# Masking the diagonal blocks of stick-breaking attention after the arithmetic instead of in the score copy

## The chip, the cores and the metric

The kernel runs on one core of one Trainium2 chip. Each run gives the time of the whole program on the device in microseconds (us). Three runs of the kernel before were timed, and one execution was profiled. TensorE (PE in the profile) multiplies matrices, VectorE (DVE), ScalarE (ACT) and GpSimd (POOL) work on tiles, SyncE (SP) issues most of the DMA transfers. Each engine runs its own list of instructions in order and waits for the others by semaphores. SBUF is the working memory, PSUM the memory that TensorE writes.

## The reference

One layer of an encoder: a layer norm, an input projection, two attention branches merged by gates, an output projection, a mixture of 64 experts and a final norm, for 1024 prompt rows and 64 sample rows with a cache of 128 keys. The change is in one branch, stick-breaking attention, with 8 heads of 128 columns:

```
z = jnp.einsum('bqhd,bkhd->bhqk', q, k).astype(F32) / math.sqrt(SB_HEAD_DIM)
mask = k_pos[None, :] < q_pos[:, None]
log_keep = jnp.where(mask, jax.nn.log_sigmoid(-z), 0.0)
after = lax.cumsum(log_keep, axis=3, reverse=True) - log_keep
log_w = jnp.where(mask, jax.nn.log_sigmoid(z) + after, 0.0)
w = jnp.where(mask, jnp.exp(log_w), 0.0)
return jnp.einsum('bhqk,bkhd->bqhd', w.astype(v.dtype), v)
```

The mask is strict: a query sees only keys before its own position.

## The kernel before

The program has stages with barriers between them: the mixer (input projection, both attention branches and their merge), a bridge (output projection, norm, router, shared expert), the experts, and the last norm. The change is in the mixer, which works head by head: first `attention(h)`, then `hgrn(h)`, the other branch.

**Units.** Scores stand with the keys on the partitions and the queries along the columns. A head has 14 units, one for each tile of 128 keys against a group of queries, listed by `attention_units`. Units 0 to 7 are queries 512 to 1023 against key tiles 7 down to 0, units 8 to 11 are queries 0 to 511 against tiles 3 down to 0, unit 12 is the 64 sample rows against themselves, and unit 13 is the same rows against the cached keys. A unit holds only the columns that can see its keys: units 0 and 8 are 128 columns wide, 1 and 9 256, 2 and 10 384, the rest 512, units 12 and 13 64. Where keys and queries meet (units 0 to 3, 8 to 11 and 12, entry 5 of the unit's tuple), the first `kr` columns are a diagonal block that needs the mask. That is 9 units of 14 in a head and 72 in all; in units 0, 8 and 12 the whole width is the diagonal block.

**One unit, step by step.** TensorE computes the scores into PSUM (`scores`, L580). VectorE brings them to SBUF as `z` (`front`, L986 and L988). In a diagonal unit this is a copy of the columns behind the block and, on the block, an addition of `cap`, a constant tile of 0 where the key is visible and -1e30 where it isn't. ScalarE takes abs, exp and ln of it (L779, L781, L783). VectorE adds max(z, 0), which gives minus log_keep, in `l` (`middle`, L997). GpSimd splits it in a high part (a cast, L1253) and a low part (a subtraction, L119 on `spl_m`). TensorE sums over the keys with a triangular matrix into PSUM (`sums`, L597 and L598) and later adds the rest of the tile for the next units (`carry`, L608 and L609). VectorE subtracts the sums from z (`back`, L1005), ScalarE takes the exponential (L789), and TensorE multiplies by the values (`values`, L625). VectorE copies finished outputs away (L1015).

**Order.** The order is written by hand. TensorE runs in step n `scores(n + 3)`, then a piece of the projections of this or the next head (`fill`, L125 to L127, of some 4 us each, absent in some steps), then `carry(n - 1)`, `sums(n)` and `values(n - 1)`. `carry` and the next `sums` wait for `arg_done`, which `back` signals. VectorE runs in step n `front(n + 3)`, `middle(n + 2)`, its part of copies of projections from PSUM (L937), `back(n)`, `outputs(n - 1)`, and in some steps whole-width work of the other branch (L1037 to L1051: its decays, and scans of them). GpSimd splits units, splits weights for the projections (L119 on `w_mix_low`), and from the second head on merges the head before (`merge`, L1230 and L1232 behind unit 3, L1236 behind unit 10, L1239 behind unit 11). In the last head there is no next head to project for, so several of TensorE's steps have no projection between their waits.

Two constant tiles matter: `before`, 1 where the key is visible and 0 elsewhere, and `cap`, made from it.

Of the kernel before, what the change touches and what calls it, by code (L numbers as in the profile page):

```python
# [17 lines left out]
ALU = mybir.AluOpType  # L18
# [307 lines left out]
def mixer(nc, a, o, xn_d, st, xT, woh, wol, ps, ident, ones, before, trir, cap, masks, lbc, small, mT_d):  # L326
    S = MixerSteps()
    UN = attention_units()
# [4 lines left out]
    Z, C, PB, OH, KE, SU = (0, 1), 2, (0, 1), 2, 3, 4  # L333
    XD = np.cumsum([0] + DIFFS).tolist()
    XE = np.cumsum([0] + EXPS).tolist()

    with ExitStack() as c:
        def sb(name, shape, dt=F32):
# [11 lines left out]
        with ExitStack() as attention_only:  # L350
            z, l = (attention_only.enter_context(nc.sbuf_tensor(n + "_m", [P, b, 512], F32)) for n, b in (("z", 5), ("l", 3)))
# [8 lines left out]
        epsc, hn = small[:, 0:1], small[:, 1:2]  # L360

        with Phase(nc, "arrived0 arrived1 rounded split mm_done act_read dve_read hn_in ck_in cv_in s_in v_out k_out s_out m_out "
                       "z_done abs_done e_done l_done z_copied sp_done hi_done lo_done c_done arg_done w_done o_done "
                       "osb_copied pa pd diff_done exp_done eb_done qe_exp qe_done x_done p_done masked a_done ke_done ke_copied "
                       "y_done oT_copied su_done s_done sg_done silu_done g_done squares root_ready u_raw merged wo_in wo_high wo_low last_s par_in xr0 xr1 xr2 xr3 var_ready rstd_ready entry_s shift_ready normed scaled xn_ready turned x_high x_low xs0 xs1 xs2 xs3 "
                       "memo built lb_in lb_act lb_dve high_ready") as (block, (
                arrived0, arrived1, rounded, split, mm_done, act_read, dve_read, hn_in, ck_in, cv_in, s_in, v_out, k_out, s_out, m_out,
                z_done, abs_done, e_done, l_done, z_copied, sp_done, hi_done, lo_done, c_done, arg_done, w_done, o_done,
                osb_copied, pa, pd, diff_done, exp_done, eb_done, qe_exp, qe_done, x_done, p_done, masked, a_done, ke_done, ke_copied,
                y_done, oT_copied, su_done, s_done, sg_done, silu_done, g_done, squares, root_ready, u_raw, merged, wo_in, wo_high, wo_low, last_s,  # L370
                par_in, xr0, xr1, xr2, xr3, var_ready, rstd_ready, entry_s, shift_ready, normed, scaled, xn_ready, turned, x_high, x_low,
# [552 lines left out]
            def _(dve):  # L924
# [44 lines left out]
                def attention(h):  # L969
# [6 lines left out]
                    def front(n):  # L976
                        kr, wd = shape(n)
                        u = u0 + n
                        dve.wait_ge(z_done, u + 1)
                        if n == 0 and h:  # L980
                            dve.wait_ge(y_done, NT * h)
                        if u >= 5:
                            dve.wait_ge(o_done, u - 4)
                        own = kr if UN[n][5] else 0
                        if own < wd:
                            mm = dve.tensor_copy(z[:kr, u % 5, own:wd], ps[:kr, Z[n % 2], own:wd])  # L986
                        if own:
                            mm = dve.tensor_tensor(z[:kr, u % 5, 0:own], ps[:kr, Z[n % 2], 0:own], cap[:kr, 0:own], ALU.add)  # L988
                        mm.then_inc(z_copied, 1)

                    def middle(n):
                        kr, wd = shape(n)
                        u = u0 + n
                        dve.wait_ge(l_done, u + 1)
                        dve.wait_ge(z_copied, u + 1)
                        lt = l[:kr, u % 3, 0:wd]
                        dve.scalar_tensor_tensor(out=lt, in0=z[:kr, u % 5, 0:wd], scalar=0.0, in1=lt, op0=ALU.max,  # L997
                                                 op1=ALU.add).then_inc(sp_done, 1)

                    def back(n):  # L1000
                        kr, wd = shape(n)
                        u, c0 = u0 + n, UN[n][4]
                        dve.wait_ge(c_done, u + 1)
                        zt = z[:kr, u % 5, 0:wd]
                        dve.tensor_tensor(zt, zt, ps[:kr, C, c0:c0 + wd], ALU.subtract).then_inc(arg_done, 1)  # L1005

                    def outputs(n):
                        if n < 0 or not UN[n][7]:
# [16 lines left out]
                    for n in range(NU + 1):  # L1025
# [9 lines left out]
                        if n == 3:  # L1035
                            dve.wait_ge(pa, PA * h + 3)
                            turn(1, dve.scalar_tensor_tensor(out=lsa[:, :], in0=A, scalar=0.0, in1=tmp[:, :], op0=ALU.min,  # L1037
                                                             op1=ALU.subtract))
# [1615 lines left out]
```

## Time and profile before

| | us |
|---|---|
| three runs, median (lowest, highest) | 2531.27 (2529.16, 2533.63) |
| the profiled execution, its own time | 2533.63 |
| its span, first to last instruction | 2531.4 |
| TensorE busy | 2357.1 |
| VectorE busy | 1463.7 |
| GpSimd busy | 1474.7 |
| ScalarE busy | 1048.3 |

The busy time of an engine over the whole span is an average over stages. What a change in one stage costs is read from that stage: which engine works without a pause there, and where it pauses, for whom. Waits are given as the time for which an engine stood idle and the instruction that ended it. Times in the rows count from the start of the span.

### The profile page before, as it was taken

How to read it: one execution, taken by the hardware profiler on the slowest of the kernel's cores; microseconds unless marked ns; L12 is line 12 of the kernel's file. 1: busy time of each engine (PE TensorE's matmuls, PEld its weight loads, DVE VectorE, ACT ScalarE, POOL GpSimd, SP SyncE). 2: the span in 40 equal slices, each digit the busy share in tenths (PEclk: the TensorE clock that was granted, in tenths of full speed). 3: DMA queues.
4: the chain of work that ended last, by engine and by line, in shares of the span. 5: the costliest groups of instructions: out<-in, count | busy, mean ns of one | idle time of the engine just before them, and what ended most of it. 6: DMA issues, size and time to landing. Idle time of an engine off the chain costs nothing. (4 is left out here: it accounts for less than half of the span.)

```text
span 2531.4 us, 38080 instructions
## 1 busy us (share of the span) xinstructions
PE 2357.1 (93%) x14242; PEld 2123.7 (84%) x14242; DVE 1463.7 (58%) x2533; ACT 1048.3 (41%) x1731; POOL 1474.7 (58%) x1526
## 2 busy tenths in 40 slices
PE   4999999999999999999999699899999999999982
PEld 4889899899898998998978487569999999989981
DVE  7375575665756656557567589534444444445334
ACT  3352733625426245254362322123444444444334
POOL 6355564665646646656465446566666677776640
PEclk9999999999999999999999799899999999999996
DMA  5201111111111110111111432399999999999995
GB/s 174 73 27 38 44 36 51 39 35 48 35 43 46 38 56 27 43 48 36 34 38 76 151 125 84 115 225 295 311 328 334 341 341 346 344 342 355 358 347 189
DMA packets 210705, 380.64 MB, mean 150 GB/s; under 512 B 25794, under 2 KB 132670, under 8 KB 210010
## 3 DMA queue, kind: packets, MB, share of 16 engines
q1 hardware_dynamic: 180330, 302.31, 33.7%
q0 software_dynamic: 30192, 75.89, 12.6%
q8 instruction: 114, 1.87, 0.3%
q14 instruction: 69, 0.57, 0.1%
HBM read 310.78 MB, written 76.41 MB: 153 GB/s over the span
## 5 line engine op out<-in xcount | busy, mean ns | idle before, releaser
L125 PE MATMUL ps<-xTh,w_mix_low 128*128 128x368 f32 (+1 forms) x1728 | 596.7, 345 | 10.1 <-POOL w_mix_low L119 8.7
L126 PE MATMUL ps<-xTl,w_mix_high 128*128 128x368 f32 (+1 forms) x1728 | 569.9, 330 | 0.0
L127 PE MATMUL ps<-xTh,w_mix_high 128*128 128x368 f32 (+1 forms) x1728 | 567.5, 328 | 0.0
L2192 POOL DMA_INDIRECT xg_early<-h_d,tabq_early x304 | 317.2, 1043 | 109.0 <-issue 86.6
L125 PEld LDWEIGHTS ps<-xTh,w_mix_low 128*128 128x128 f32 x1728 | 326.5, 189 | 21.5 <-issue 18.2
L126 PEld LDWEIGHTS ps<-xTl,w_mix_high 128*128 128x128 f32 x1728 | 326.7, 189 | 9.1 <-issue 6.3
L127 PEld LDWEIGHTS ps<-xTh,w_mix_high 128*128 128x128 f32 x1728 | 326.1, 189 | 0.0
L2204 POOL DMA_INDIRECT ys_d<-yo,tab_early x114 | 210.1, 1843 | 173.5 <-DMA ys_d<-yo,tab_early 79.9
L1273 POOL TENSOR_TENSOR x_m<-x_m,kh_m 128x128 f32<-128x128 f32 (+1 forms) x272 | 128.2, 471 | 215.5 <-ACT x_m L830 215.5
L119 POOL TENSOR_TENSOR w_mix_low<-w_mix_raw,w_mix_high 128x1024 fp32r<-128x1024 f32 x72 | 182.0, 2528 | 88.4 <-ACT w_mix_high L114 88.0
L119 DVE TENSOR_TENSOR wdl<-wd_early,wdh 128x2048 fp32r<-128x2048 f32 x64 | 146.7, 2293 | 134.0 <-ACT wdh L114 81.6
L2233 PEld LDWEIGHTS ps<-xgT,wg_early 128*128 128x128 f32 x1376 | 182.7, 192 | 11.2 <-issue 6.7
L2305 ACT ACTIVATE yo<-ps,wcol 128x512 f32<-128x512 f32 x228 | 156.4, 686 | 83.4 <-PE ps L127 28.9
L2233 PE MATMUL ps<-xgT,wg_early 128*128 128x144 f32 (+6 forms) x1376 | 184.5, 293 | 5.8 <-DVE xgT L2330 5.8
L2233 PE MATMUL ps<-xgT,wu_early 128*128 128x144 f32 (+6 forms) x1376 | 182.1, 291 | 0.0
L2233 PEld LDWEIGHTS ps<-xgT,wu_early 128*128 128x128 f32 x1376 | 177.8, 190 | 0.0
L1253 POOL CAST sph_m<-l_m 128x128 fp32r<-128x128 f32 (+3 forms) x112 | 68.1, 608 | 173.3 <-PE ps L598 132.9
L2341 DVE SCALAR_TENSOR_TENSOR yo<-ps,wcol,yo 16x512 f32<-16x512 f32 (+5 forms) x100 | 74.0, 740 | 144.2 <-ACT yo L2305 127.8
L1073 DVE TENSOR_TENSOR x_m<-bT_m 128x128 f32<-128x128 f32 (+1 forms) x544 | 147.5, 347 | 0.0
L1090 DVE TENSOR_REDUCE aT_m<-pm_m 128x128 f32<-128x1024 f32 (+1 forms) x72 | 135.7, 1884 | 2.5
L114 ACT ACTIVATE hTh<-hT 128x256 fp32r<-128x256 f32 x64 | 26.8, 418 | 264.9 <-DVE hT L2363 206.0
L114 ACT ACTIVATE wdh<-wd_early 128x2048 fp32r<-128x2048 f32 x64 | 122.4, 1912 | 25.6 <-DMA wd_early<-in_w_exp_down 21.0
(365 smaller groups left out, 4942.6 us busy)
## 6 DMA issues: line engine op xcount, KB each, us to landing
wd_early<-in_w_exp_down SPq DMA_DIRECT2D x64, 1024.0 KB
wg_early<-in_w_exp_gate SPq DMA_DIRECT2D x82, 512.0 KB
wu_early<-in_w_exp_up SPq DMA_DIRECT2D x82, 512.0 KB
w_mix_raw<-in_w_in SPq DMA_DIRECT2D x72, 512.0 KB, 3.8
wg<-in_w_exp_gate SPq DMA_DIRECT2D x42, 512.0 KB
wu<-in_w_exp_up SPq DMA_DIRECT2D x42, 512.0 KB
xg_early<-h_d,tabq_early POOLq DMA_INDIRECT x316
mT_d<-gs_m SPq DMA_DIRECT2D x8, 544.0 KB, 2.7
```

The lines of the kernel that those rows point to most:

```text
L114: return act.activation(hi, x, ACT.Copy)
L119: return dve.tensor_tensor(lo, x, hi.bitcast(F32), ALU.subtract)
L125: pe.matmul(out, ll, rh, start=start, stop=False)
L126: pe.matmul(out, lh, rl, start=False, stop=False)
L127: return pe.matmul(out, lh, rh, start=False, stop=stop)
L1073: dve.tensor_tensor(xs, *((mid, bs) if side == 0 else (bs, mid)), ALU.subtract).then_inc(diff_done, 1)
L1090: dve.tensor_reduce(aT[:m, j % 2, 0:m], pm[:m, j % 2, 0:s, 0:m].rearrange("p l t -> p t l"), AX.X, ALU.add).then_inc(a_done, 1)
L1273: pool.tensor_tensor(xs, xs, seg(q, LEVELS[i], side), ALU.mult).then_inc(x_done, 1)
L2192: pool.indirect_dma_start(out=xg[:, b, g, :], out_offset=None, in_=h2_d[:, :].rearrange("t (q n) -> (t q) n", q=4), in_offset=bass.Indirec ...
L2204: pool.indirect_dma_start(out=ys_d[:, :], out_offset=rows_of(e, j, m), in_=yo[:m, b, j, :], in_offset=None, compute_op=ALU.add, bounds_che ...
L2233: mm = pe.matmul(ps[:, bank[e % 2], f * cap:(f + 1) * cap], raw[e % DEEP][:, k, f * P:(f + 1) * P], xT[:, e % 2, k, 0:cap], start=k == 0, ...
L2305: act.activation(yo[:m, b, j, q * 512:(q + 1) * 512], ps[part, DB[n], :], ACT.Copy, scale=wcol[part, b, j:j + 1]).then_inc(y_ready, 1)
```

## The change

The front of a diagonal unit becomes one copy of the full width without a mask. The mask is applied twice later, on the diagonal block alone and by VectorE: in `middle` a multiplication by `before` makes the terms of the hidden keys 0, and in `back` a minimum with `cap` sends their exponents to -1e30. Each new operation reads what the one in front of it wrote, so each waits for it on a semaphore of its own (`sp_raw`, `arg_raw`), and the signal for the other engines (`sp_done`, `arg_done`) moves behind the new operation. Nothing changes in the lists of TensorE, ScalarE, GpSimd and SyncE.

```diff
+    diag = [n for n, u in enumerate(UN) if u[5]]
...
-                        own = kr if UN[n][5] else 0
-                        if own < wd:
-                            mm = dve.tensor_copy(z[:kr, u % 5, own:wd], ps[:kr, Z[n % 2], own:wd])
-                        if own:
-                            mm = dve.tensor_tensor(z[:kr, u % 5, 0:own], ps[:kr, Z[n % 2], 0:own], cap[:kr, 0:own], ALU.add)
-                        mm.then_inc(z_copied, 1)
+                        dve.tensor_copy(z[:kr, u % 5, 0:wd], ps[:kr, Z[n % 2], 0:wd]).then_inc(z_copied, 1)
...
-                        dve.scalar_tensor_tensor(out=lt, in0=z[:kr, u % 5, 0:wd], scalar=0.0, in1=lt, op0=ALU.max,
-                                                 op1=ALU.add).then_inc(sp_done, 1)
+                        mm = dve.scalar_tensor_tensor(out=lt, in0=z[:kr, u % 5, 0:wd], scalar=0.0, in1=lt, op0=ALU.max, op1=ALU.add)
+                        if UN[n][5]:
+                            mm.then_inc(sp_raw, 1)
+                            dve.wait_ge(sp_raw, len(diag) * h + diag.index(n) + 1)
+                            mm = dve.tensor_tensor(lt[:, 0:kr], lt[:, 0:kr], before[:kr, 0:kr], ALU.mult)
+                        mm.then_inc(sp_done, 1)
...
-                        dve.tensor_tensor(zt, zt, ps[:kr, C, c0:c0 + wd], ALU.subtract).then_inc(arg_done, 1)
+                        mm = dve.tensor_tensor(zt, zt, ps[:kr, C, c0:c0 + wd], ALU.subtract)
+                        if UN[n][5]:
+                            mm.then_inc(arg_raw, 1)
+                            dve.wait_ge(arg_raw, len(diag) * h + diag.index(n) + 1)
+                            mm = dve.tensor_tensor(zt[:, 0:kr], zt[:, 0:kr], cap[:kr, 0:kr], ALU.min)
+                        mm.then_inc(arg_done, 1)
```

## Rows read from the trace of the kernel before

**Rows 1.** The page, part 1: busy us, share of the span, instructions.

```profile
PE 2357.1 (93%) x14242; PEld 2123.7 (84%) x14242; DVE 1463.7 (58%) x2533; ACT 1048.3 (41%) x1731; POOL 1474.7 (58%) x1526
```

**Rows 2.** Busy us of each engine by stretch, then clock, DMA share, GB/s.

```profile
105.00:1421.00 1316.00, 1263.84 (x7617) 1164.91 (x7617) 843.87 (x1493) 590.43 (x1009) 756.05 (x932) 0.99 0.14 42
...
438.00:605.00 167.00, 163.24 (x991) 151.27 (x991) 105.07 (x186) 74.28 (x127) 96.02 (x118) 1.00 0.14 41
...
1273.00:1421.00 148.00, 122.47 (x695) 106.98 (x694) 112.26 (x192) 72.30 (x125) 94.83 (x118) 0.91 0.15 54
```

**Rows 3.** TensorE's waits, 100 to 1421 us: total, times, longest.

```profile
PE ps L125 <- POOL w_mix_low L119: 8.7, 7, 1.3
PE ps L608 <- DVE z_m L1005: 7.8, 3, 3.9
PE ps L625 <- ACT z_m L789: 7.5, 14, 0.7
PE ps L580 <- DVE z_m L988: 3.5, 1, 3.5
```

**Rows 4.** VectorE's groups by shape: busy us, mean ns, idle before.

```profile
L1073 DVE TENSOR_TENSOR x_m<-bT_m 128x128 f32<-128x128 f32 x448 | 137.1, 381 | 0.0
...
L988 DVE TENSOR_TENSOR z_m<-ps,cap 128x128 f32<-128x128 f32 x64 | 18.1, 283 | 0.8
```

**Rows 5.** VectorE's timeline, two places: start us, length us, instruction, idle before.

```profile
504.95 2.91 DVE L1073 TENSOR_TENSOR x_m<-bT_m 128x128 f32<-128x128 f32 x14
...
1357.64 1.23 DVE L1086 TENSOR_TENSOR pm_m<-ps,masks 128x1024 f32<-128x1024 f32 x1 [1.24 <-PE ps L656]
1358.91 1.97 DVE L1090 TENSOR_REDUCE aT_m<-pm_m 128x128 f32<-128x1024 f32 x1
```

**Rows 6.** Timeline of VectorE and GpSimd, 473 to 486 us.

```profile
473.11 2.30 POOL L119 TENSOR_TENSOR spl_m<-l_m,sph_m 128x512 fp32r<-128x512 f32 x1
...
474.71 0.85 DVE L997 SCALAR_TENSOR_TENSOR l_m<-z_m,l_m 128x128 f32<-128x128 f32 x1
...
483.29 0.56 DVE L986 COPY z_m<-ps 128x384 f32<-128x384 f32 x1
483.76 0.28 DVE L988 TENSOR_TENSOR z_m<-ps,cap 128x128 f32<-128x128 f32 x1
483.96 1.94 DVE L997 SCALAR_TENSOR_TENSOR l_m<-z_m,l_m 128x384 f32<-128x384 f32 x1
```

**Rows 7.** Timeline around `back` of unit 2 in the third head.

```profile
455.78 0.56 DVE L1005 TENSOR_TENSOR z_m<-z_m,ps 128x384 f32<-128x384 f32 x1 [2.87 <-PE ps L598]
455.90 2.53 POOL L1232 TENSOR_TENSOR gh_m<-gh_m,oT_m 128x1088 f32<-128x1088 f32 x1
...
457.20 0.62 PE L608 MATMUL ps<-spl_m,trir 128*128 128x384 f32 x1
```

**Rows 8.** Timeline, units 9 and 11 of the same head.

```profile
490.87 0.67 DVE L997 SCALAR_TENSOR_TENSOR l_m<-z_m,l_m 128x512 f32<-128x512 f32 x1
491.46 0.53 DVE L937 COPY hq_m<-ps 128x368 f32<-128x368 f32 x1
...
491.60 0.61 POOL L1253 CAST sph_m<-l_m 128x512 fp32r<-128x512 f32 x1 [1.05 <-DVE l_m L997]
...
491.91 0.40 DVE L1005 TENSOR_TENSOR z_m<-z_m,ps 128x256 f32<-128x256 f32 x1
...
492.29 1.77 POOL L119 TENSOR_TENSOR spl_m<-l_m,sph_m 128x512 fp32r<-128x512 f32 x1
...
493.82 0.28 PE L608 MATMUL ps<-spl_m,trir 128*128 128x256 f32 x1
...
499.69 0.69 DVE L1005 TENSOR_TENSOR z_m<-z_m,ps 128x512 f32<-128x512 f32 x1 [0.29 <-PE ps L598]
...
501.10 0.70 PE L625 MATMUL ps<-z_m,vrow_m 128*128 128x512 f32 x1
```

**Rows 9.** TensorE's timeline in the last head, `carry` of unit 10.

```profile
1332.40 0.69 PE L608 MATMUL ps<-spl_m,trir 128*128 128x384 f32 x1 [2.51 <-DVE z_m L1005]
```

More of the change, by code:

```diff
@@ L362, in mixer @@
         with Phase(nc, "arrived0 arrived1 rounded split mm_done act_read dve_read hn_in ck_in cv_in s_in v_out k_out s_out m_out "
-                       "z_done abs_done e_done l_done z_copied sp_done hi_done lo_done c_done arg_done w_done o_done "
+                       "z_done abs_done e_done l_done z_copied sp_raw sp_done hi_done lo_done c_done arg_raw arg_done w_done o_done "
                        "osb_copied pa pd diff_done exp_done eb_done qe_exp qe_done x_done p_done masked a_done ke_done ke_copied "
@@ L367, in mixer @@
                 arrived0, arrived1, rounded, split, mm_done, act_read, dve_read, hn_in, ck_in, cv_in, s_in, v_out, k_out, s_out, m_out,
-                z_done, abs_done, e_done, l_done, z_copied, sp_done, hi_done, lo_done, c_done, arg_done, w_done, o_done,
+                z_done, abs_done, e_done, l_done, z_copied, sp_raw, sp_done, hi_done, lo_done, c_done, arg_raw, arg_done, w_done, o_done,
                 osb_copied, pa, pd, diff_done, exp_done, eb_done, qe_exp, qe_done, x_done, p_done, masked, a_done, ke_done, ke_copied,
```

## Prediction

> **What bounds the kernel now.** I read the page's busy times first [rows 1]: TensorE is busy for 93% of the span, VectorE for 58%. Then the table by stretch [rows 2]. The changed code runs only in the mixer, some 105 to 1421 us. There TensorE is busy 1263.84 of 1316 us, and over a middle head (438 to 605 us) 163.24 of 167. So TensorE sets the mixer, and VectorE, busy 105.07 us of that head, costs time only where TensorE stands still for it. The list of TensorE's waits shows where it does now [rows 3]: 8.7 us for a weight split on GpSimd, 7.8 us in three waits for the subtraction at L1005, 7.5 us for the exponential behind it, 3.5 us for the front at L988. All small. The question is whether the added work uses up the slack between VectorE and the TensorE instructions that read its results. The later stages begin after a barrier, so what attention loses is lost at the end one to one.
>
> **What an added operation costs.** Nine of a head's 14 units are diagonal, 72 in all. Each loses an addition at the front (L988, inputs in PSUM and SBUF, mean 283 ns) and gains two operations with both inputs in SBUF: the multiplication in `middle`, the minimum in `back`, 144 in all. No row shows these; the nearest is L1073, the same class and size, 14 of which take 2.91 us undisturbed, 0.21 each from start to start [rows 4, 5]. But each new one waits for the one before it. L1090 waits for L1086 [rows 5] and starts 1358.91 - (1357.64 + 1.23) = 0.04 us after its end (0.03 unrounded), where unwaited neighbours overlap by 0.07. So an added operation is 0.28 + 0.03 = 0.31 us in its chain. L1073's mean over all 448 is 381 ns, because some are held up; that is the second and larger cost.
>
> The Trainium skill (VectorE: DVE Perf Modes, section "The DRAIN you can't avoid") says that a semaphore after every Vector operation costs nothing extra. The rows disagree, 0.31 against 0.21; by the rule the 144 operations are 30 us of VectorE's time, by the rows 45. The same page (section on the TRN2 errata) gives 58 cycles plus the width for SBUF inputs, 120 for PSUM; by it the added operation would be 0.06 us shorter than the removed one. Undisturbed, the trace has them equal, and the measurement decides.
>
> **The hold-up by GpSimd.** An operation with both inputs in SBUF does not run while a tensor_tensor of GpSimd does [rows 6]. `middle` of unit 8, 128 columns wide, is issued at 474.71; GpSimd's split of unit 7 ends at 473.11 + 2.30 = 475.41; the VectorE operation ends at 474.71 + 0.85 = 475.56, so 0.15 us behind it, where alone it would have ended at 475.00. `middle` of unit 10 (1.94 us for 384 columns) is held in the same way, while L986, L988 and L1005, which read PSUM, keep their length beside GpSimd (L1005 at 455.78 runs into L1232 and still takes 0.56 us for 384 columns [rows 7]). So the change moves work out of the class that is never held into the one that is. A held 128-column operation ends 0.15 us behind GpSimd.
>
> **What is removed.** In three diagonal units of nine the tile is as wide as the diagonal block, and a copy replaces an addition of equal length. In the other six a copy and an addition become one wider copy: for unit 11 from 483.29 to 483.96, 0.67 [rows 6], against some 0.61 to 0.69 for 512 columns at once. I take 0.07 each and nothing on the path, since after unit 1 TensorE is still streaming unit 2's scores; the bound is the 3.5 us of L580 in rows 3.
>
> **First place: unit 2, heads 1 to 7** [rows 7]. `back` of unit 2 ends at 455.78 + 0.56 = 456.34, and TensorE reads its result at L608 at 457.20. The new minimum is issued at 456.37. But GpSimd began the merge product L1232 at 455.90, and that runs to 458.43. The minimum ends at 458.58, L608 starts 0.05 later (a semaphore's way): 458.63 - 457.20 = 1.43 us of stall. Behind the minimum stand on VectorE the copy of unit 6's scores and `middle` of unit 5, on ScalarE the exponential of unit 2 and the three passes over `tmp`; TensorE needs each of them more than 1 us later than they come, and its own reads move back too. The merge runs in heads 1 to 7: 7 x 1.43 = 10.0 us. Were the minimum not held, it would end at 456.65, within the 0.87 us of slack: 0.
>
> **Second place: unit 9** [rows 8]. The multiplication of unit 11 follows `middle`, and both queues go on from its end. Today, from the end of `middle` (491.54), GpSimd's cast starts 0.06 later, lasts 0.61, and its subtraction starts 0.08 after that: 0.75. VectorE copies a projection (it starts 0.08 before the mark, 0.45 to the next start), does `back` of unit 9 (0.40) and would issue the minimum 0.03 later: 0.80. So GpSimd is first by 0.05 us, and the minimum is held for the 1.29 us that this subtraction takes when free (the 1.77 of the row is itself held). The mark moves by 0.31 for its own multiplication and some 0.34 for unit 10's multiplication and unit 8's minimum, passed on through GpSimd's subtraction and L1048: 492.19. The subtraction ends at 492.94 + 1.29 = 494.23, the minimum at 494.38; TensorE wants it at 493.82. With the 0.05, 0.6 us of stall in heads 1 to 6: 3.6 us. A race that falls the other way gives 0.
>
> **Third place: unit 11** [rows 8]. Its `back` starts 0.04 us behind TensorE's sums, after 0.29 of idle time that swallows the lateness before it, and the values of that unit (L625 at 501.10) wait for its exponential (among the 14 such waits of rows 3). One minimum is 0.31 us in full: 6 x 0.31 = 1.9 us.
>
> **Heads 0 and 7.** Head 0 has no merge; I charge it one operation at unit 11 and 0.2 at unit 2: 0.5 us. In head 7 no projections of a next head lie between the units, and TensorE waits for `back` three times already, the last time 2.51 us before 1332.40 [rows 9]. Ahead of that stand three added multiplications and three minima, 6 x 0.31 less 0.07 at the front: 1.8 us.
>
> **Sum.** 10.0 + 3.6 + 1.9 + 0.5 + 1.8 = 17.8 us. The profiled execution took 2533.63 us, 2.2 more than its span, and would take 2551.4. The median of the three runs, 2531.27, is 2.4 lower: 2549 us, +0.7%. The disputed term is held or not held, and I take held: L1232 is 0.47 us into its run when the minimum arrives, no close race.
>
> **Rivals.**
> - *Nothing is held up*: a short operation slips in. Then plain lengths count alone: 1.9 + 0.5 + 1.8 = 4.2 us, 2535.5 us, +0.17%, within the 0.2% (5 us) that a measurement of this kernel can tell from no change. For it: the held operation of rows 6 is a scalar_tensor_tensor, and of the new kind, a tensor_tensor on a constant tile, no row shows one beside GpSimd. Against: L1073's mean of 381 ns, which is of that kind and above its free length.
> - *The second race falls to VectorE*: 17.8 - 3.6 = 14.2 us, 2545.5 us; it turns on 0.05 us. If a waiting operation could start without the 0.11 us that rows 5 show, this is what would happen. The skill's rule on free semaphores, above, would give that.
> - *The clock falls.* Head 7's stretch has a granted clock of 0.91 on average, against 1.00 in a middle head [rows 2]: 27 of its 148 us at 1.2 GHz instead of 2.4. Put down to its three waits in rows 3, that is 9 us and 4.5 us lost for a wait of 2.6; in proportion 2.5 us for each stall of 1.43, seven times, 17 us more: 2566 us. Against: the waits for the weight split, up to 1.3 us in seven heads, leave the clock at 1.00.
> - *Faster: the front counts, the additions hide.* If all of the time from L988 to the next instruction (0.20, rows 6) were won in 48 units and the added work lay in VectorE's idle time, that is 9.6 us: 2521.7 us. It decides only where the minima are not read at once; rows 7 and 8 show that they are.
>
> **Chances.** As summed (2546 to 2556) 0.64, race to VectorE 0.12, clock 0.08, nothing held 0.12, faster 0.04: slower 0.84, no change 0.12, faster 0.04. The range reaches from just above the unheld case, 2536, to 2560 for later waits that I priced at nothing; it leaves out the clock case, the faster one and half of the unheld one.
>
> **What would show it.** The minimum of unit 2 should last some 2.2 us in seven heads and end 0.15 us behind L1232. TensorE should show seven waits at L608 of about 1.4 us for it and six of 0.6 for unit 9's, and its waits at L625 should grow by 0.3 each. The waits after attention (L125 for the split) should stay as they are, and so should the later stages. I am wrong if the minimum of unit 2 lasts 0.28 us, if the clock of heads 1 to 6 falls below 1.00, or if a head makes the stall up later.

## The result, and the profile after

The kernel after takes 2554.76 us (median of four runs, 2551.97 to 2561.36), the kernel before 2531.49 (four runs, 2529.16 to 2533.63). The ratio is 1.0083, with a 95% interval of 1.0068 to 1.0097: slower by 17 to 25 us. The forecast was 2549, the range 2536 to 2560.

The profiled execution took 2553.7 us with a span of 2549.3. Busy times, from the first part of its page, to hold against [rows 1]:

```profile
PE 2357.6 (92%) x14242; PEld 2119.0 (83%) x14242; DVE 1522.8 (60%) x2629; ACT 1049.5 (41%) x1731; POOL 1449.4 (57%) x1526
```

VectorE has 96 instructions more (144 added, 48 fewer at the front) and is busy for 59 us more, TensorE for as long as before. 25 us fewer are shown for GpSimd: its operations too are longer or shorter by what they are held.

The table by stretch, for the mixer and for the third head, with the columns of [rows 2]:

```profile
102.00:1438.00 1336.00, 1267.72 (x7617) 1163.82 (x7617) 907.22 (x1589) 592.41 (x1009) 740.56 (x936) 0.99 0.14 41
438.00:607.00 169.00, 163.41 (x992) 150.76 (x991) 113.42 (x198) 74.41 (x127) 93.69 (x118) 1.00 0.14 41
```

TensorE does the same 163 us of work in the third head, in 169 us instead of 167, at a granted clock of 1.00 in both (2.4 GHz, where 0.50 is 1.2 GHz). TensorE's waits in the mixer, which answer to [rows 3]:

```profile
PE ps L609 <- DVE z_m L1009: 18.7, 16, 4.0
PE ps L653 <- DVE pm_m L1091: 10.7, 10, 1.2
PE ps L125 <- POOL w_mix_low L119: 8.9, 7, 1.3
PE ps L626 <- ACT z_m L790: 8.8, 21, 0.7
...
PE ps L581 <- DVE z_m L985: 3.5, 1, 3.5
```

Three waits for `back` became sixteen for the minimum behind it: seven in unit 2, six in unit 9, and the three of the last head. The waits for the weight split and the one at the front stay. So do the ten waits for VectorE in `hgrn` (L653), 10.7 us before as well; they are the largest total before, and [rows 3] leave them out. VectorE's groups, for [rows 4]:

```profile
L1078 DVE TENSOR_TENSOR x_m<-bT_m 128x128 f32<-128x128 f32 x448 | 137.3, 385 | 0.0
L1009 DVE TENSOR_TENSOR z_m<-z_m,cap 128x128 f32<-128x128 f32 x64 | 46.6, 728 | 2.2
...
L997 DVE TENSOR_TENSOR l_m<-l_m,before 128x128 f32<-128x128 f32 x64 | 18.7, 292 | 2.2
```

The multiplication is never held: 292 ns on average, and none longer than 0.30 us. The minimum takes 728 ns on average. Where the difference sits is seen in the timeline around unit 2 of the third head, the place of [rows 7]:

```profile
455.93 0.56 DVE L1005 TENSOR_TENSOR z_m<-z_m,ps 128x384 f32<-128x384 f32 x1 [2.87 <-PE ps L599]
...
456.05 2.48 POOL L1237 TENSOR_TENSOR gh_m<-gh_m,oT_m 128x1088 f32<-128x1088 f32 x1
...
456.52 2.16 DVE L1009 TENSOR_TENSOR z_m<-z_m,cap 128x128 f32<-128x128 f32 x1
...
458.73 0.44 PE L609 MATMUL ps<-spl_m,trir 128*128 128x384 f32 x1 [0.93 <-DVE z_m L1009]
```

The merge product ends at 456.05 + 2.48 = 458.53, the minimum at 456.52 + 2.16 = 458.68, which is 0.15 behind it, and `carry` starts 0.05 later. Unit 9 of the same head, for [rows 8]:

```profile
492.44 0.67 DVE L993 SCALAR_TENSOR_TENSOR l_m<-z_m,l_m 128x512 f32<-128x512 f32 x1
...
493.14 0.29 DVE L997 TENSOR_TENSOR l_m<-l_m,before 128x128 f32<-128x128 f32 x1
...
493.80 0.41 DVE L1005 TENSOR_TENSOR z_m<-z_m,ps 128x256 f32<-128x256 f32 x1
494.19 1.28 POOL L119 TENSOR_TENSOR spl_m<-l_m,sph_m 128x512 fp32r<-128x512 f32 x1
494.24 1.37 DVE L1009 TENSOR_TENSOR z_m<-z_m,cap 128x128 f32<-128x128 f32 x1
...
495.67 0.39 PE L609 MATMUL ps<-spl_m,trir 128*128 128x256 f32 x1 [0.54 <-DVE z_m L1009]
```

GpSimd's subtraction starts at 494.19, the minimum is issued at 494.24: GpSimd was first by 0.05 us. A held minimum costs nothing by itself: in head 0 those of units 3 and 9 last 1.78 and 1.38 us, and TensorE waits for neither. And the last head's three waits, of which [rows 9] shows the third:

```profile
1334.19 0.48 PE L609 MATMUL ps<-spl_m,trir 128*128 128x128 f32 x1 [2.29 <-DVE z_m L1009]
...
1340.18 0.58 PE L609 MATMUL ps<-spl_m,trir 128*128 128x256 f32 x1 [4.02 <-DVE z_m L1009]
...
1345.31 0.69 PE L609 MATMUL ps<-spl_m,trir 128*128 128x384 f32 x1 [2.84 <-DVE z_m L1009]
```

**Where the time went.** From the first score product of a head (L580, now L581) to that of the next, in us; the column of head 7 runs from the last head's first score product to the first transfer of the next stage, and the sum of the eight is called the mixer:

| head | 0 | 1 to 6, mean | 7 | mixer |
|---|---|---|---|---|
| before | 169.46 | 167.16 | 148.03 | 1320.42 |
| after | 169.78 | 169.20 | 151.44 | 1336.43 |
| difference | 0.32 | 2.04 | 3.41 | 16.0 |

The profiled executions differ by 20.1 us. 16.0 are in the mixer, 2.0 in what lies before and behind it in the span, and 2.1 outside the span: 2553.7 - 2549.3 = 4.4 us after, 2.3 before. Each figure of this table, and of the one below, is of one profiled execution.

### The profile page after: what moved, and what is told of

It reads as the page before. It is cut to its first block and busy times, and to the rows that moved or that the text cites. A ratio compares the mean times of both kernels' runs of the same rounds, so it can differ in the third digit from the quotient of the medians.

```text
span 2549.3 us, 38176 instructions
## 1 busy us (share of the span) xinstructions
PE 2357.6 (92%) x14242; PEld 2119.0 (83%) x14242; DVE 1522.8 (60%) x2629; ACT 1049.5 (41%) x1731; POOL 1449.4 (57%) x1526
## 5 line engine op out<-in xcount | busy, mean ns | idle before, releaser
L2197 POOL DMA_INDIRECT xg_early<-h_d,tabq_early x304 | 310.6, 1022 | 135.0 <-issue 75.0
L119 POOL TENSOR_TENSOR w_mix_low<-w_mix_raw,w_mix_high 128x1024 fp32r<-128x1024 f32 x72 | 174.8, 2428 | 88.3 <-ACT w_mix_high L114 88.0
L1258 POOL CAST sph_m<-l_m 128x128 fp32r<-128x128 f32 (+3 forms) x112 | 60.1, 537 | 202.4 <-PE ps L599 138.4
L1078 DVE TENSOR_TENSOR x_m<-bT_m 128x128 f32<-128x128 f32 (+1 forms) x544 | 147.8, 350 | 0.0
```

The lines of the kernel that those rows point to most:

```text
L119: return dve.tensor_tensor(lo, x, hi.bitcast(F32), ALU.subtract)
L1078: dve.tensor_tensor(xs, *((mid, bs) if side == 0 else (bs, mid)), ALU.subtract).then_inc(diff_done, 1)
L2197: pool.indirect_dma_start(out=xg[:, b, g, :], out_offset=None, in_=h2_d[:, :].rearrange("t (q n) -> (t q) n", q=4), in_offset=bass.Indirec ...
```

## The experiments

Four kernels at a time ran on one chip together with the kernel before, whose median was 2516.6 us in the first group, 2536.9 in the second and 2535.9 in the third. So a time is compared only with the kernel before of its own group. Most times of one kernel on one chip lie within 5 us of their median, but in the second and third group single ones lie 9 to 11 us off it (the kernel before, back first, early minimum, both moved, early addition, last merge late), while the mixer of the kernel before came out as 1320.42 and 1320.39. So I read the effect of an edit from the mixer and its heads, and give the ratio beside it. All of it in one table ("low" is the time that TensorE has a granted clock of 0.5 in the last head's first two such stretches, in us, "out" the median of time minus span). Two kernels have no ratio: their output differs so much that the experts' stage does other work, with 44589 and 39938 instructions profiled in place of after's 38176, and their whole times, 3602.7 us for multiplication only and 2790.1 us for front only, can't be held against the others.

```
kernel               ratio to before           head 0  1-6 mean  head 7  mixer    low          out
before, again        1.0006 [0.9996, 1.0015]   169.48  167.17    147.90  1320.39  13.6 +  6.8  2.0
after                1.0083 [1.0068, 1.0097]   169.78  169.20    151.44  1336.43  17.1 + 10.2  4.7
merge later          1.0043 [1.0026, 1.0060]   170.76  168.32    149.99  1330.63  13.6 + 10.2  4.5
minimum only         1.0045 [1.0029, 1.0062]   170.57  168.69    150.64  1333.36  13.7 + 10.2  2.1
multiplication only  (experts differ)          169.63  167.28    149.54  1322.82  13.6 + 10.2  1.7
back first           1.0048 [1.0028, 1.0068]   170.56  168.66    151.15  1333.67  13.7 + 10.2  4.7
early minimum        0.9994 [0.9979, 1.0009]   169.52  167.11    149.94  1322.10  17.1 + 10.2  2.0
both moved           1.0016 [1.0001, 1.0031]   169.74  167.52    150.62  1325.47  17.1 + 10.2  4.9
two minima           1.0198 [1.0172, 1.0225]   171.95  174.24    152.90  1370.29  17.1 + 10.2  2.1
early addition       1.0012 [1.0003, 1.0021]   169.38  167.12    150.30  1322.42  17.0 + 10.2  2.0
last merge late      0.9979 [0.9968, 0.9991]   170.27  167.33    147.39  1321.65   6.8 +  3.4  2.0
padded               1.0072 [1.0057, 1.0087]   170.67  169.43    150.72  1337.98  13.6 +  6.8  3.0
front only           (experts differ)          169.49  167.17    149.29  1321.79  17.1 + 10.2  1.7
```

**The kernel before, again.** No edit; it tells how far two measurements of one kernel differ.

> The kernel before, run again beside the others, for its span and its time outside the span. The mixer of the changed kernel grew by 16.0 us from first scores to the transfer that opens the next stage, its span by 17.9, its median by 23.3. Theory: the 5 us beyond the mixer are spread between executions (of the later stages and of what lies outside the span), so this control should show spans that vary by some 3 to 5 us too, and a time outside the span between 2 and 5 us. Rival: the changed program really is slower outside the mixer; then this control has its 2.2 us outside the span every time.

Ratio 1.0006, mixer 1320.39. Every head is within 0.22 us of the first profile, and the mean of heads 1 to 6 within 0.01; in the kernel with the last merge late, which has the same code there, that mean is 0.16 higher. So a head's figure, and a mean of six, can be trusted to some 0.2. The spans of its ten executions reach from 2511 to 2520 us, as the theory wants. But the time outside the span is 1.9 to 2.3 us in all ten, as the rival wants: what after has there beyond it isn't spread between executions.

**The merge one unit later.** In the kernel after, the whole of the first merge step of GpSimd moves from behind unit 3 to behind unit 4. It tells whether the merge product holds the minimum of unit 2.

```diff
-                        if h and n in (3, 10, 11):
-                            merge(h - 1, (3, 10, 11).index(n))
+                        if h and n in (4, 10, 11):
+                            merge(h - 1, (4, 10, 11).index(n))
```

> The changed kernel, with GpSimd's merge step 0 (L1230, L1232) moved from behind unit 3 to behind unit 4, nothing else. Held theory: the minimum of unit 2 falls to 0.3 us, TensorE's wait of 0.93 us before its L608 goes in heads 1 to 7, and the time falls by about 7 x 1.2 = 8.4 us, unless the moved merge holds another VectorE operation that has less than 1 us of slack. Length theory (the minimum and its semaphore simply take this long in the chain): nothing changes, within 1 us.

The mechanism is there; VectorE and GpSimd at unit 2 of the third head in the timeline of this kernel:

```profile
456.43 0.61 POOL L1258 CAST sph_m<-l_m 128x512 fp32r<-128x512 f32 x1 [3.53 <-PE ps L599]
456.92 0.29 DVE L1009 TENSOR_TENSOR z_m<-z_m,cap 128x128 f32<-128x128 f32 x1
...
457.76 0.62 PE L609 MATMUL ps<-spl_m,trir 128*128 128x384 f32 x1
```

The minimum takes 0.29 us instead of 2.16, and `carry` doesn't wait. The gain is smaller than I expected: 0.88 us in each of heads 1 to 6 and 1.45 in head 7, 5.8 in the mixer in place of 8.4. The moved merge brings no new wait of TensorE. Head 0 is 1.0 us longer, of which the granted clock explains most: it is 0.5 there for 6.8 us instead of 3.4, and `carry` of unit 1 is late by 0.8 already. No merge runs in head 0.

**The minimum alone.** The multiplication is left out, so the terms of the hidden keys go into the sums, and the output differs. It tells whether the second place needs the lateness of both added operations.

```diff
                         mm = dve.scalar_tensor_tensor(out=lt, in0=z[:kr, u % 5, 0:wd], scalar=0.0, in1=lt, op0=ALU.max, op1=ALU.add)
-                        if UN[n][5]:
-                            mm.then_inc(sp_raw, 1)
-                            dve.wait_ge(sp_raw, len(diag) * h + diag.index(n) + 1)
-                            mm = dve.tensor_tensor(lt[:, 0:kr], lt[:, 0:kr], before[:kr, 0:kr], ALU.mult)
                         mm.then_inc(sp_done, 1)
```

> The changed kernel without the multiplication in middle (the hidden keys then add to the sums, so the output differs). Held theory: the minimum of unit 2 is still held and costs its 1.2 to 1.4 us in seven heads, the minimum of unit 9 is held too but ends some 0.6 us earlier and costs almost nothing, unit 11 costs its 0.3, and head 7 half of its 1.8: about 4.5 us less than the changed kernel. Length theory (144 equal operations): half of the loss goes, some 11 us less.

Heads 1 to 6 are 0.51 us shorter each, and `carry` of unit 9 no longer waits (10 waits at L609 in place of 16), though the minimum is held as before (1.38 us): GpSimd's subtraction begins 0.65 us earlier in the head, as its input does, and so the minimum ends before TensorE wants it. Unit 2 keeps its 2.17 us. The mixer is 3.1 us shorter in place of 4.5, and 0.8 of the difference is again head 0 at the lower clock.

**The multiplication alone.** The minimum is left out, so hidden keys keep their weights. The output differs, and only the mixer can be read.

```diff
-                        if UN[n][5]:
-                            mm.then_inc(arg_raw, 1)
-                            dve.wait_ge(arg_raw, len(diag) * h + diag.index(n) + 1)
-                            mm = dve.tensor_tensor(zt[:, 0:kr], zt[:, 0:kr], cap[:kr, 0:kr], ALU.min)
```

> The changed kernel without the minimum in back (the hidden keys then enter the product with the values, so the output differs). Held theory: every stall of heads 1 to 6 goes, only head 7 keeps some 0.9 us: the time is 1 to 3 us above the kernel before. Length theory: half of the loss stays, some 11 us above it.

The mixer is 2.4 us above that of before, 1.5 of it in head 7 and 0.12 in each of heads 1 to 6. So the multiplication by itself costs a middle head nothing that can be told from the 0.2 us above: what it feeds is wanted more than its 0.3 us later.

**`back` before the projection copy, in step 9.** It moves the minimum of unit 9 some 0.5 us forward in VectorE's list, so that it wins the race against GpSimd's subtraction.

```diff
-                        evacuate(*S.attn[h][n])
+                        if n != 9:
+                            evacuate(*S.attn[h][n])
                         if n < NU:
                             back(n)
+                        if n == 9:
+                            evacuate(*S.attn[h][n])
```

> The changed kernel with one exchange on VectorE in step 9 of a head: back of unit 9 and its minimum come before the copy of the projection, not behind it. Race theory: the minimum is issued 0.45 us earlier, before GpSimd's subtraction for unit 11 begins, and is held by the cast alone. TensorE's wait of 0.53 us before its L608 for unit 9 goes in heads 1 to 6, its mixer gets 3 to 3.5 us shorter. Lateness theory (VectorE is simply behind by then): the wait shrinks by the copy's 0.45 us and unit 11 gives part of it back, some 1 to 2 us in all.

Its timeline at unit 9 of the third head:

```profile
493.56 0.41 DVE L1005 TENSOR_TENSOR z_m<-z_m,ps 128x256 f32<-128x256 f32 x1
...
494.00 0.46 DVE L1009 TENSOR_TENSOR z_m<-z_m,cap 128x128 f32<-128x128 f32 x1
...
494.40 1.30 POOL L119 TENSOR_TENSOR spl_m<-l_m,sph_m 128x512 fp32r<-128x512 f32 x1
```

The minimum is issued 0.40 us before the subtraction and lasts 0.46, not 1.37. Heads 1 to 6 get 0.54 us shorter each, 3.3 in all, as the theory of the race wants. The whole mixer is 2.8 us shorter; head 0 is 0.8 longer, with 6.8 us at a granted clock of 0.5 in place of 3.4.

**The same operations, early.** All 144 added operations stay, but the minimum moves from `back` to right behind the multiplication in `middle`, two steps before its result is wanted. A minimum there cuts the positive scores of visible keys in the diagonal blocks to 0, so the output differs. In that place it also waits for nothing that was written just before it. It sets the theory that the place costs the time against the theory that the length of the added work does.

```diff
+                            zd = z[:kr, u % 5, 0:kr]
-                            mm = dve.tensor_tensor(lt[:, 0:kr], lt[:, 0:kr], before[:kr, 0:kr], ALU.mult)
+                            dve.tensor_tensor(lt[:, 0:kr], lt[:, 0:kr], before[:kr, 0:kr], ALU.mult).then_inc(sp_done, 1)
+                            dve.tensor_tensor(zd, zd, cap[:kr, 0:kr], ALU.min).then_inc(arg_raw, 1)
+                            return
...
                         if UN[n][5]:
-                            mm.then_inc(arg_raw, 1)
                             dve.wait_ge(arg_raw, len(diag) * h + diag.index(n) + 1)
-                            mm = dve.tensor_tensor(zt[:, 0:kr], zt[:, 0:kr], cap[:kr, 0:kr], ALU.min)
+                        mm = dve.tensor_tensor(zt, zt, ps[:kr, C, c0:c0 + wd], ALU.subtract)
```

> The changed kernel with the minimum with cap moved from back to middle, where VectorE lowers z itself right behind the multiplication, before the sums are there (the value that reaches the exponential is as low). The number of operations is the same. Held theory: no added operation stands between TensorE's sums and its next read any more; places one to three go, heads 1 to 6 are as before, and the mixer is 2 to 3 us longer than before for head 7 alone (13 to 14 us shorter than the changed kernel's). Length theory (VectorE has too much to do): the mixer stays over 10 us longer than before.

TensorE's waits in the mixer are those of before again, but for 0.9 us in the last head:

```profile
PE ps L609 <- DVE z_m L1010: 8.7, 3, 4.0
PE ps L626 <- ACT z_m L790: 7.5, 14, 0.7
```

The mixer is 14.3 us shorter than after's and 1.7 above that of before, heads 1 to 6 are equal to before's. The place decides, not the length of the added work.

**Both moves together**: the merge one unit later and `back` first in step 9, the two diffs above.

> The changes of the two kernels with the merge behind unit 4 and with back before the copy in step 9 together. Additive theory: the mixer gets 5.8 us (first, measured; head 0 had 0.8 us of chance in it) plus 3 to 3.5 us shorter than the changed kernel's, to some 6 to 7 us above before, of which unit 11's 0.3 us in seven heads and head 7's 1.8 to 3 are left, and 0.3 us of lateness a head. Rival: the stalls cover each other, and the second gives less than 1 us here.

Heads 1 to 6 are 1.68 us shorter, against 0.88 and 0.54 by the single moves: the two places add up, with 0.26 more. Told from the other side, moving the merge when `back` is already first gains 1.14 us a head, and moving `back` when the merge is already later 0.80. The mixer is 5.1 us above before, less than the 6 to 7 expected. What is left above before in a middle head is 0.35 us: the third place.

**Two minima.** The minimum is done twice over, each waiting for the one before.

```diff
-                            mm.then_inc(arg_raw, 1)
-                            dve.wait_ge(arg_raw, len(diag) * h + diag.index(n) + 1)
-                            mm = dve.tensor_tensor(zt[:, 0:kr], zt[:, 0:kr], cap[:kr, 0:kr], ALU.min)
+                            for again in (0, 1):
+                                mm.then_inc(arg_raw, 1)
+                                dve.wait_ge(arg_raw, 2 * (len(diag) * h + diag.index(n)) + 1 + again)
+                                mm = dve.tensor_tensor(zt[:, 0:kr], zt[:, 0:kr], cap[:kr, 0:kr], ALU.min)
```

> The changed kernel with the minimum done twice, each waiting for the one before (same output). Held theory: the second minimum finds GpSimd just freed or itself waiting, and costs its plain 0.31 us: units 2 and 9 and 11 of the middle heads cost 0.3 more each, head 7 three times 0.3, together 6 to 8 us more in the mixer. Length theory (a minimum at unit 2 costs the 2.16 us that it lasts): another 2 us for unit 2 alone in seven heads, 15 us or more in all.

This was a plain miss: a mixer 34 us longer than after's. At unit 2 the second minimum adds 0.23 us to TensorE's wait, near the 0.3 that I expected. At unit 9 it doesn't, as this kernel's timeline shows in the fourth head:

```profile
678.26 1.28 POOL L119 TENSOR_TENSOR spl_m<-l_m,sph_m 128x512 fp32r<-128x512 f32 x1
678.32 3.85 DVE L1010 TENSOR_TENSOR z_m<-z_m,cap 128x128 f32<-128x128 f32 x2
679.49 2.52 POOL L1245 TENSOR_TENSOR gs_m<-gs_m,gh_m 128x1088 f32<-128x1088 f32 x1
...
682.22 0.39 PE L609 MATMUL ps<-spl_m,trir 128*128 128x256 f32 x1 [3.25 <-DVE z_m L1010]
```

The row with x2 is both minima. The first is held by the subtraction, which ends at 679.54, and ends 0.15 behind it, at 679.68. GpSimd's next product is recorded from 679.49 on, so it is ahead of the second minimum, which is issued at 679.72 and ends at 682.17, 0.16 behind the product's end. Two operations with a wait between them pay here for two operations of GpSimd, and TensorE waits 3.25 us. And now the clock follows:

```profile
660.00:683.00 23.00, 19.11 (x102) 16.24 (x101) 19.53 (x28) 12.60 (x23) 13.27 (x12) 1.00 0.09 26
683.50:686.90 3.40, 3.40 (x14) 3.40 (x13) 1.66 (x6) 1.15 (x4) 0.41 (x2) 0.51 0.21 84
```

Some 1.2 us behind the wait of 3.25 the granted clock is at its lower level, 1.2 GHz, for 3.4 us, in each of heads 3 to 6 (6.8 us in head 2), where after has 1.00. Head 1 has the same wait (3.29), no such stretch, and is 1.5 us shorter than heads 3 to 6, so the length of the wait alone doesn't tell. Of the 5.0 us that a middle head loses against after, 3.6 are waits, as in head 1, and 1.4 to 1.5 the clock, as an estimate from the difference of these heads.

**The same operations early, as an addition.** As "early minimum", with `ALU.add` in place of `ALU.min` (the hidden scores get -1e30, as in the kernel before, but after ScalarE has read them). This is the change in full, in another place.

> As the kernel with the early minimum, but cap is added instead, which leaves positive visible scores alone, so this is a full version of the change. Place theory: the mixer is 1.5 to 2 us longer than before (all in head 7), the whole time within 0.2% of before.

Mixer 1322.42, heads 1 to 6 as before, ratio 1.0012. It takes back all of the stalls that after has in heads 1 to 6 and gains nothing over before: the front isn't where time is lost. The 2.0 us that the mixer is above before's are in head 7.

**The last head's merge later.** In the kernel before, merge steps 1 and 2 of the last head move behind units 12 and 13.

```diff
-                        if h and n in (3, 10, 11):
-                            merge(h - 1, (3, 10, 11).index(n))
+                        at = (3, 10, 11) if h < HEADS - 1 else (3, 12, 13)
+                        if h and n in at:
+                            merge(h - 1, at.index(n))
```

> The kernel before, with the last two merge steps of head 7 moved from behind units 10 and 11 to behind units 12 and 13. Held theory: in head 7 the scan behind unit 8 (2.58 us) and middle of unit 12 (2.31 us) are no longer held, back of units 9 and 10 come 2 us or more earlier, and TensorE, which waits for them there, gets 2 to 4 us of the mixer back, if the clock does not change. Rival: the merge then holds VectorE's later operations and nothing is won, within 0.5 us.

TensorE's waits for `back` in the last head of this kernel:

```profile
1321.82 0.33 PE L608 MATMUL ps<-spl_m,trir 128*128 128x128 f32 x1 [1.43 <-DVE z_m L1005]
...
1325.35 0.58 PE L608 MATMUL ps<-spl_m,trir 128*128 128x256 f32 x1 [2.42 <-DVE z_m L1005]
...
1328.03 0.69 PE L608 MATMUL ps<-spl_m,trir 128*128 128x384 f32 x1 [0.39 <-DVE z_m L1005]
...
1335.63 0.29 PE L608 MATMUL ps<-spl_m,trir 64*128 64x64 f32 x1 [1.43 <-DVE z_m L1005]
```

The second and third wait shrink by 1.3 and 2.1 us, a fourth of 1.43 appears (the rival has a part in it), and attention of the last head ends 1.9 us sooner. But only 0.5 of it is left at the end of the head. It is lost right behind attention, where this kernel has its second stretch at the lower clock and the kernel before has none; first this kernel, then the kernel before in its second profile, over the same stretch:

```profile
1337.30:1340.70 3.40, 3.40 (x14) 3.40 (x13) 3.24 (x16) 1.06 (x1) 0.15 (x1) 0.50 0.00 0
```

```profile
1337.30:1340.70 3.40, 3.40 (x22) 3.40 (x22) 3.33 (x16) 1.06 (x1) 0.23 (x1) 1.00 0.00 0
```

The third stretch, from 1402 us on, lasts 30.7 us in place of 6.8 and 20.5, and changes the head by less than 0.2 us. With a ratio of 0.9979 (12 runs against 23) this is the one version clearly below both kernels, yet the mixer of the profiled execution, which was the slowest of the twelve, isn't shorter, 1321.65. Where the 5 us of the ratio come from isn't shown.

**The kernel after, padded.** One wait that is long satisfied in each of the 72 score steps of `hgrn`. It was to tell whether the 2.7 us more outside the span follow the length or place of the code.

```diff
+                        dve.wait_ge(z_copied, NU * (h + 1))
```

> The changed kernel with one more wait in each of VectorE's 72 score steps of the other branch, on a semaphore that has long been reached. Layout theory: the 2.6 us that the changed kernel takes outside its span (4.7 against 2.0, seen in the kernels with exactly its number of instructions, not in two with 72 more nor in one with 72 fewer) fall to 2.0; the mixer stays as in the changed kernel, within 1 us. Rival: they stay at 4.7, and belong to what these kernels do, not to their length.

Time minus span is 3.0 us, neither after's 4.7 nor before's 2.0, with the stalls unchanged (heads 1 to 6 within 0.23 us). Inconclusive as to the cause. One thing more comes out of it: its operations are after's, and yet its last head has 13.6 and 6.8 us at the lower clock where after's has 17.1 and 10.2, and is 0.7 us shorter.

**The front alone.** Both added operations are left out, so nothing is masked; only the mixer can be read.

```diff
-                        if UN[n][5]:
-                            mm.then_inc(sp_raw, 1)
-                            dve.wait_ge(sp_raw, len(diag) * h + diag.index(n) + 1)
-                            mm = dve.tensor_tensor(lt[:, 0:kr], lt[:, 0:kr], before[:kr, 0:kr], ALU.mult)
...
-                        if UN[n][5]:
-                            mm.then_inc(arg_raw, 1)
-                            dve.wait_ge(arg_raw, len(diag) * h + diag.index(n) + 1)
-                            mm = dve.tensor_tensor(zt[:, 0:kr], zt[:, 0:kr], cap[:kr, 0:kr], ALU.min)
```

> The changed kernel without the multiplication and without the minimum, so without any mask in the diagonal blocks (the output differs, and with it the routing and the time of the later stages; only the mixer is to be read). Theory: the one copy in place of copy and addition is worth nothing in heads 0 to 6 and at most 0.5 us in head 7. Rival: the front counts, and the mixer gets up to 9.6 us shorter than before.

Heads 1 to 6 take 167.17 us, as before's in its second profile: the cheaper front is worth nothing. Head 7 takes 1.3 us *more*, although its waits are as before's. The stretches explain it, first for the kernel before in its second profile, then for this kernel:

```profile
1319.60:1333.20 13.60, 7.23 (x21) 5.41 (x22) 12.46 (x18) 4.26 (x12) 10.15 (x10) 0.50 0.10 42
...
1401.50:1408.30 6.80, 4.83 (x11) 3.25 (x12) 5.85 (x8) 2.75 (x7) 6.72 (x3) 0.50 0.07 19
```

```profile
1319.10:1336.20 17.10, 10.49 (x28) 7.26 (x29) 13.77 (x21) 4.96 (x13) 10.21 (x10) 0.50 0.08 34
...
1401.30:1411.50 10.20, 7.18 (x16) 4.27 (x16) 9.22 (x11) 5.15 (x11) 10.04 (x4) 0.51 0.04 13
```

The granted clock stays at the lower level for 3.4 us longer in each of two places. In the first of them products run at it that have 1.00 in the kernel before, and TensorE is 1.5 us late behind them, where it was not late in front of them.

## Why the prediction came out right, and where it didn't

**What bounds the kernel, and that the places count.** Right. With the same 144 operations the mixer is at 1336.4 or at 1322.1, by where the minimum stands.

**The price of an added operation, 0.31 us in its chain.** Right. The multiplication of unit 11 starts 0.03 us behind `middle` (492.44 + 0.67 = 493.11, then 493.14) and takes 0.29. The Trainium skill (VectorE: DVE Perf Modes, section "The DRAIN you can't avoid") has the semaphore between two operations for free, measured there on a copy. It doesn't hold here: the trace after has L1078, without waits, still at 0.21 from start to start, and the waiting ones at 0.32.

**First place, unit 2.** The mechanism is right to the digit: seven minima of 2.15 to 2.17 us, ending 0.15 behind the merge product, and `carry` 1.38 us later in its head than before (forecast 1.43; in the third head 1.46, but 0.09 of it is there before unit 2). The size is off, because I took the late start for the loss. Before, the product at L608 was let in while the one ahead of it was still running, and so is shown as 0.62 us long [rows 7]; now it starts alone and takes 0.44, and TensorE's wait is shown as 0.93 us, not as the 1.4 that I named as a sign. What is lost is at its end, and the next `carry` is 1.11 us late in each of the seven heads. So the term of 10.0 measured 7 x 1.11 = 7.8. The experiment that takes it away gave back 5.3 + 1.45 = 6.8 by itself, and 1.14 a head where unit 9 had been mended before it. The Trainium skill (SBUF — State Buffer, section "SBUF: two separate sides") says that the port pair shared by VectorE and GpSimd is taken for a whole instruction, by the one that starts first, when the VectorE operation has two SBUF inputs and the GpSimd one reads SBUF. The minimum of unit 2 agrees, 2.16 us beside the product and 0.29 without it.

**Second place, unit 9.** The mechanism is right: the race is lost by 0.05 us, and the stall is shown as 0.45 to 0.54 in six heads. The size came out above the forecast of 3.6. From `carry` of unit 8 to the first sums of unit 10 the lateness grows by 0.71 to 0.82 us in heads 1 to 6, 4.7 in all. Moving `back` gives back 3.3 by itself and 6 x 0.80 = 4.8 where the merge had been moved before it; leaving out the multiplication gives back 3.1. The rival that VectorE wins the race is refuted in after, and shown as possible with 0.40 us of lead.

**Third place, unit 11.** Right: 0.33 us a head measured, 0.31 forecast. TensorE's waits for the exponential grew from 14 to 21, by 1.3 us in all. With both other places removed 0.35 us a head is left.

**Head 0.** 0.3 us, forecast 0.5.

**Head 7.** 3.4 us in all against 1.43 + 1.8 = 3.2, but made of other parts. Unit 2 makes TensorE 1.11 us late. Its three waits grow by 0.85, 0.12 and 0.33, 1.3 us together, not 1.8, and behind the third it is 2.6 us late. The rest comes from the clock, which I had as a rival for all heads and priced at nothing here. Products behind the third wait that had a granted clock of 1.00 before have 0.50 after, first before, then after:

```profile
1336.42 1.12 PE L625 MATMUL ps<-z_m,vrow_m 128*128 128x512 f32 x2
```

```profile
1349.80 1.53 PE L626 MATMUL ps<-z_m,vrow_m 128*128 128x512 f32 x2
```

Over these and their neighbours the lateness grows from 2.57 to 3.44, by 0.9 us. Whether the change brings this longer stretch isn't shown, since the padded kernel, with the same operations, doesn't have it.

**Sum.** By the lateness of TensorE the terms are 7.8 + 4.7 + 2.0 + 0.3 + 2.3 = 17.1 us. Heads 1 to 6 make up 1.0 of it again, half between units 2 and 8 and half behind attention, which leaves 16.1 against 16.0 measured. The forecast was 17.8. That it is so near has some luck in it: the first term was 2.2 too high, the second and the last head's together 1.6 too low, and that a head makes a part of its stall up, which I had named as a sign of being wrong, was priced at nothing.

That the median came out 5.8 us above the forecast isn't due to these steps. Time minus span is 4.7 us in the median over 21 runs of the kernel after, and 2.0 for before: 2.7 us that the sum took as fixed ("2.2 more than its span"). That leaves 4.6 us (23.3 - 16.0 - 2.7) for the span outside the mixer, where the profiled executions show 2.0 and where executions of one kernel differ by as much. Most of that is likely the scatter of four runs, though it isn't shown. All 21 executions of the kernel after on record have a median of 2551.9 us, 2.9 below that of the four; against the same 2531.5 the difference would be 20.4, and 1.7 would be left. And the padded kernel, 18.8 us above the kernel before of its group, has 17.6 of it in the mixer and 1.1 outside the span, which leaves next to nothing. The step that failed is the one that the sum never wrote down: that a difference in the mixer is the whole difference. The time outside the span, 2.7 us, is the part of it that the runs show.

**The rivals.** Nothing held: refuted, 728 ns on average. Faster by the front: refuted, the front alone is worth 0.0 in a middle head. The clock: heads 1 to 6 stay at 1.00, with stalls of 0.93 and 0.54 us. Its price was also about twice too high, for it put all of the 27 us at the lower clock down to the three waits; the trace has 13.7 us at them, and the others are in two stretches from 1404 us on. But it is no empty case: one more minimum, a wait of 3.25 us, and it comes, 1.4 to 1.5 us a head.

## What to carry to other kernels

Before adding a short VectorE operation with two SBUF inputs, look in the timeline for what GpSimd runs at that moment: where the result is wanted at once, the price is what is left of that operation, not 0.3 us, and a second operation that waits for the first can pay for the next one of GpSimd too. Put such an operation where its result is wanted a step later; here the same 144 operations cost 16 us in one place and 2 in another. And read the effect from the stage it is in, since the whole time moves by several us from execution to execution, and with the code by some us that no engine shows.

## What the runs showed that I had not expected

- **Turns.** Where GpSimd runs one operation right behind the other, its next one is ahead of a VectorE operation that has to wait for the one before it: 72 more minima of 0.3 us each cost 34 us of the mixer, with what the clock takes of it.
- **Casts hold too.** A minimum beside GpSimd's cast of the split takes 0.40 to 0.48 us instead of 0.29 (units 0, 1 and 8 of the third head). In unit 0 the cast ends at 445.63 and the minimum at 445.78, 0.15 behind it, as beside a product:

```profile
445.13 0.50 POOL L1258 CAST sph_m<-l_m 128x384 fp32r<-128x384 f32 x1 [1.81 <-PE ps L599]
...
445.36 0.42 DVE L1009 TENSOR_TENSOR z_m<-z_m,cap 128x128 f32<-128x128 f32 x1
```

- **The clock at the lower level.** With the front alone no wait of TensorE changes, and yet two such stretches of the last head are longer, 13.6 to 17.1 and 6.8 to 10.2 us, which costs 1.3 us. Whether the edit does it or chance isn't shown, with one profile of it. In the kernel before, the first of these stretches begins at 1322.1, 0.2 us behind a wait of 1.44 us; in the kernel with two minima head 1 keeps 1.00 behind a wait of 3.29. In head 0 there are 3.4 us at the lower level or 6.8, in kernels that don't differ there (before and last merge late): the head takes 169.4 to 169.8 us with the one and 170.3 to 170.8 with the other (two minima aside). An effect below 1 us in such a head is no evidence.
- **Time outside the span.** The four kernels with 38176 instructions in the profile (after, merge later, back first, both moved) have 4.5 to 4.9 us there, the padded one with 38178 has 3.0, and all others, with 38080 to 44589, have 1.7 to 2.1. What sets it stays open.
